# A two-block transformer kernel: squares of X moved behind the splits, tables loaded later

## Chip, core and metric

The kernel runs on one core of one Trainium2 chip. The metric is device time in microseconds (us) of one execution. The kernel before takes 1373.84 us, the median of 3 runs (1373.65 to 1375.49).

## What is computed

A 512 x 1024 activation `x` goes through two transformer blocks. The first is a mixer with a global and a windowed attention and a SiLU FFN, the second a pooling mixer, a stick-breaking attention, an FFN and a gated projection of a second input `p`. Only the opening matters here:

```
h = rms_norm(x, norm_mix_pre)        # x * rsqrt(mean(x*x) + EPS) * gain
proj = h @ w_in                      # 1024 -> 1536 columns
qa, ka, va, qb, kb, vb = split(proj)
qa, ka = rope(rms_norm(qa)), rope(rms_norm(ka));  qb, kb = rope(qb), rope(kb)
...                                  # attentions, FFN, the whole second block
x = x + sigmoid(rms_norm(x) @ w_ple_gate) * (p @ w_ple_proj)
```

## The kernel before

Everything is transposed: `X` holds 8 tiles of 128 features x 512 positions. Matrices are read in units of 16 blocks of 128x128 (`w_raw`, three slots in turn). For near-fp32 accuracy each operand is split into a high part of type fp32r (ScalarE, `w_hi`, `h_hi`) and the remainder (VectorE, `w_lo`, `h_lo`), and each product is three matmuls (`three`): hi x hi, lo x hi and hi x lo.

The order of work is written out by hand, one program for each engine, with semaphores between them. An engine executes its instructions strictly in that order, so an instruction that waits holds up all that stands behind it. The opening goes so:

- **SP** queues the loads: X in five parts (`X_PARTS`), between them the first weight unit in quarters, then units 1 and 2, all without a wait. Unit 3 waits until the matmuls of unit 0 are done.
- **ACT** (L906 to L934) loads gains, `ident` and `ones` on its own DMA queue. Then for each of 8 tiles it makes `h_hi[k] = X[k] * gain`, every second time the high part of a weight quarter, issues the load of `c1` after the first quarter (1.25 MiB: a matrix for head sums, one for rotation, attention masks, and cosines and sines), and squares the tile before. The squares go to the two buffers of `sq` in turn, so `square` waits at L866 until POOL has added the one two before. Behind the eighth come the load of `p` into `hf`, `split(1)` (the high part of unit 1), the high part of `p`, and rounded copies of `ident` and of the masks. Then the loop over the 12 output chunks evacuates (`evacuate`), splits later units and finishes heads.
- **POOL** adds squares 1 to 7 into `sqsum` (`sum_squares`, L418); the eighth is taken directly by TensorE.
- **DVE** makes `h_lo` and the low quarters, `split(1)`, the low part of `p`, `split(2)`, then the statistics (`variance`, `factors`), and from L1415 on the normed and rotated heads (`rope`), which share their cosine and sine tables in `c1`.
- **PE** runs `first_units` (chunks 0 and 1 together, feature tile by feature tile, as they arrive), then chunk 2 out of unit 1. After chunk 2 `beside(2)` calls `total`: with `ones` as right side it sums `sqsum` and the last square over partitions (16 matmuls of one column), and takes up `item(0)` and `item(1)` (a transpose, head sums, a rotation). Three feature tiles into chunk 3 `eps_row` makes the row that DVE waits for at L1415.

`F1`, which the change uses, is an 8-tile buffer that later holds the mixer's output. It lies where the query tiles `QA` lie, which are first written after the first rotated query.

Of the kernel before, what the change touches and what calls it, by code (L numbers as in the profile page):

```python
# [12 lines left out]
P = 128  # L13
KD = D // P
# [51 lines left out]
C1_AT = C_INVC + 4 * PADW  # L66
C_HONE, C_ROT, C_MASK = C1_AT, C1_AT + P, C1_AT + 2 * P
# [20 lines left out]
def build(nc, xT, pT, weights, gains, consts, outT):  # L88
# [5 lines left out]
    ACT = mybir.ActivationFunctionType  # L94
# [4 lines left out]
    with ctx:  # L99
# [258 lines left out]

        X_PARTS = [(0, 1), (1, 2), (2, 4), (4, 6), (6, 8)]

        def landed(u):
            return raw_landed[u % SLOTS], 16 * (u // SLOTS + (u % SLOTS > 0))

# [44 lines left out]
        @block.gpsimd  # L408
        def _(pool):
            def sum_squares(nm):  # L410

                if nm.before is not None:
                    pool.wait_ge(*nm.before.total(1))
                nc.gpsimd.memset(sqsum[:, :], 0.0).then_inc(nm.summed.sem, 1)
                for j in range(nm.sums - 1):
                    pool.wait_ge(*nm.squares(j + 1))
                    pool.wait_ge(*nm.summed(j + 1))
                    nc.gpsimd.tensor_tensor(sqsum[:, :], sqsum[:, :], sq[:, j % 2, :], ALU.add  # L418
                                            ).then_inc(nm.summed.sem, 1)

            def zero_masked(t):

                for at in (0, 512, 896, 1024):
                    v = t[:, at:at + P]
                    last = nc.gpsimd.affine_select(out=v, in_=v, compare_op=ALU.is_gt, fill=0.0, base=0,
                                                   pattern=[[1, P]], channel_multiplier=-1)
                return last

            n_self = [0]

            def link(ins):

                n_self[0] += 1
                ins.then_inc(pool_self, 1)
                pool.wait_ge(pool_self, n_self[0])

            def low_qk(j):

                c = ORDER1[j]
                last = None  # L440
                for i in range(2):
                    if last is not None:
                        link(last)
                    pool.wait_ge(roped_hi, 2 * ROPED.index(c) + i + 1)
                    rows, other = slice(HD * i, HD * i + HD), slice(HD * (1 - i), HD * (1 - i) + HD)
                    t = y_of(j)[rows, :]
                    if c in (4, 10):
                        k = KA if c == 4 else KB
                        hi = k[rows, 0, i, :]
                        link(nc.gpsimd.tensor_tensor(k[rows, 1, i, :], t, hi.bitcast(f32), ALU.subtract))  # L450
                        last = nc.gpsimd.tensor_tensor(k[other, 1, i, :], t, hi.bitcast(f32), ALU.subtract)
                    else:
                        q, h = (QA, 2 * c + i) if c in NORMED else (QB, 2 * (c - 6) + i)
                        last = nc.gpsimd.tensor_tensor(q[other, h, :], t, q[rows, h, :].bitcast(f32), ALU.subtract)
                last.then_inc(rope_done, 1)
                pool.wait_ge(rope_done, ROPED.index(c) + 1)

            sum_squares(n_mix_pre)
            for j in range(len(ORDER1)):
                if ORDER1[j] not in V1:  # L460
                    low_qk(j)
            for nm in norms[1:7]:
                sum_squares(nm)
            for h in range(NH):
                pool.wait_ge(sp_ready, h + 1)
                zero_masked(E2[:, h % 2, :]).then_inc(sp_masked, 1)
            for nm in norms[7:]:
                sum_squares(nm)
# [3 lines left out]
        def _(pe):  # L472
# [58 lines left out]
            def total(nm):  # L531

                if nm.before is None:
                    pe.wait_ge(c0_landed, 32)
                for src, ready, n in ((sqsum[:, :], nm.summed, nm.n), (sq[:, (nm.n - 1) % 2, :], nm.squares, nm.n)):
                    pe.wait_ge(*ready(n))
                    for b in range(NB):
                        last = mm(ps[:, nm.ss_bank, b:b + 1], src[:, b * P:(b + 1) * P], ones[:, 0:1],
                                  ready is nm.summed and b == 0, True, loose=True)
                last.then_inc(nm.total.sem, 1)  # L540
# [311 lines left out]
        def _(act):  # L852
# [8 lines left out]
            def af(out, in_, func, **kw):  # L861
                return nc.scalar.activation(out, in_, func, **kw)  # L862

            def split(u):

                slot, width = u % SLOTS, tiles_of(u)  # L866
                act.wait_ge(*landed(u))
                af(w_hi[slot][:, 0:width * P], w_raw[slot][:, 0:width * P], ACT.Copy).then_inc(hi_ready, 1)

            def square(nm, j, src):  # L870
                if j >= 2:
                    act.wait_ge(*nm.summed(j))
                af(sq[:, j % 2, :], src, ACT.Square).then_inc(nm.squares.sem, 1)

            def tables(name):

# [33 lines left out]
            for k in range(KD):  # L910
                if k < 2 or k % 2 == 0:
                    act.wait_ge(x_landed[k if k < 2 else k // 2 + 1], 16)
                af(h_hi[:, k, :], X[:, k, :], ACT.Copy, scale=gcol("norm_mix_pre", k)).then_inc(n_mix_pre.hi.sem, 1)
                if k % 2 == 0:
                    act.wait_ge(first_landed[k // 2], 16)
                    af(quarter(w_hi[0], k // 2), quarter(w_raw[0], k // 2), ACT.Copy).then_inc(first_hi, 1)
                if k == 0:
                    act.dma_start(c1[:, :], consts[:, C1_AT:]).then_inc(c1_landed, 16)
                else:
                    square(n_mix_pre, k - 1, X[:, k - 1, :])  # L920
            square(n_mix_pre, KD - 1, X[:, KD - 1, :])
            act.dma_start(hf[:, :, :], pT.rearrange("(k p) s -> p k s", p=P)).then_inc(p_landed, 16)
            split(1)
            act.wait_ge(p_landed, 16)
            af(p_hi[:, :, :], hf[:, :, :], ACT.Copy).then_inc(p_hi_ready, 1)


            def finish(j):
                c = ORDER1[j]
                if c in V1:  # L930
                    act.wait_ge(vtr_done, V1.index(c) + 1)
                    act.wait_ge(*n_mix_pre.diag(1))
                    for b in range(NB):
                        last = af((VA if c == 5 else VB)[:, b, :], ps[:, rot_bank(j), b * P:(b + 1) * P], ACT.Copy,  # L934
                                  scale=stat[:, 3, b:b + 1])
                    last.then_inc(v_ready, 1)
                elif c in NORMED:
                    act.wait_ge(hvar_ready, NORMED.index(c) + 1)
                    link(af(rt[:, 3, :], rt[:, 2, :], ACT.Ln))
                    af(rt[:, 3, :], rt[:, 3, :], ACT.Exp, scale=-0.5).then_inc(hguess_ready, 1)  # L940

            def high_qk(j):
# [13 lines left out]
                           ACT.Copy)  # L956
                    af(dst, y_of(j)[rows, :], ACT.Copy).then_inc(roped_hi, 1)

            act.wait_ge(c0_landed, 32)
            act.wait_ge(c1_landed, 16)  # L960
            af(ident_r[:, :], ident[:, :], ACT.Copy).then_inc(masks_ready, 1)
            af(mask_r[:, :, :], c1[:, C_MASK - C1_AT:C_MASK - C1_AT + 2 * P].rearrange("p (m c) -> p m c", m=2),
               ACT.Copy).then_inc(masks_ready, 1)

            def evacuate(j):

                c = ORDER1[j]
# [15 lines left out]
            for j in range(12):  # L983
                if j in (3, 5, 7, 9):
                    split(j // 2 + 2)
                evacuate(j)
                if j == 1:
                    split(2)
                if j == 2:
                    guess(n_mix_pre)  # L990
                    finish(0)
                    finish(1)
                if 3 <= j <= LATE1:
                    finish(j - 1)
                if 3 <= j < LATE1 + 2:
                    high_qk(j - 2)
# [247 lines left out]
        def _(dve):  # L1244
# [24 lines left out]
            def split(u):  # L1269

                slot, width = u % SLOTS, tiles_of(u)
                dve.wait_ge(hi_ready, u)
                low(w_lo[slot][:, 0:width * P], w_raw[slot][:, 0:width * P], w_hi[slot][:, 0:width * P]
                    ).then_inc(lo_ready, 1)
# [79 lines left out]
            for k in range(KD):  # L1354
                late_low(n_mix_pre, "norm_mix_pre", k)
                if k % 2 == 0:
                    dve.wait_ge(first_hi, k // 2 + 1)
                    low(quarter(w_lo[0], k // 2), quarter(w_raw[0], k // 2), quarter(w_hi[0], k // 2)
                        ).then_inc(first_lo, 1)
            split(1)  # L1360
            dve.wait_ge(p_hi_ready, 1)
            low(p_lo[:, :, :], hf[:, :, :], p_hi[:, :, :]).then_inc(p_lo_ready, 1)
            split(2)
            dve.wait_ge(c0_landed, 32)
            variance(n_mix_pre)
            dve.wait_ge(*n_mix_pre.var(1))
# [367 lines left out]
```

## Time and profile before

| | |
|---|---|
| median of 3 runs | 1373.84 us (1373.65 to 1375.49) |
| the profiled execution's own time | 1378.3 us |
| its span | 1376.5 us |
| mean granted TensorE clock | 0.988 |
| busy: PE, PEld, DVE, ACT, POOL | 97%, 78%, 50%, 40%, 11% of the span |

PE is the matmul pipe of TensorE, PEld its weight loads, DVE is VectorE, ACT ScalarE, POOL GpSimd, SP the engine that issues most DMAs; ACTq and SPq rows are their issues of DMAs. A name such as `ps<-h_hi,w_hi` is output and inputs; numbers of buffers are left out, and so `F1` is shown as `F`. The clock is a fraction of full speed. The two levels that occur are 0.50 (1.2 GHz) and 1.00 (2.4 GHz). In a bracket behind a row stands how long the engine was idle before it and what ended that.

### The profile page before, as it was taken

To read this page: it belongs to the slowest core of one execution; us is meant where nothing else is said; L and a number is where in the kernel's file an instruction comes from. 1 tells how busy PE (TensorE), PEld (TensorE's weight loads), DVE (VectorE), ACT (ScalarE), POOL (GpSimd) and SP (SyncE) were. 2 spreads that over 40 slices of the span, in tenths; PEclk is the share of its full clock that TensorE was granted. 3 is DMA by queue.
4 is the path that set the end of the run, shared out by engine and by line. 5 is a ranking of instruction groups with operands and counts; after the bars stand their busy time and mean duration, and the time that the engine had idled before them with its cause. 6 is when DMAs were issued, how large, how long until landed. Compare 5 with 4: busy or idle time off the path is not lost.

```text
span 1376.5 us, 14683 instructions
## 1 busy us (share of the span) xinstructions
PE 1329.5 (97%) x6056; PEld 1066.9 (78%) x6056; DVE 694.8 (50%) x907; ACT 546.1 (40%) x733; POOL 150.3 (11%) x136
## 2 busy tenths in 40 slices
PE   7987989999999999999999999999999999999995
PEld 5764657888888888887888777888888888888874
DVE  6998773665444442126534455563544354423254
ACT  6558864543233222225224555542423232222232
POOL 3351012510000000103000001012000000010021
PEclk9999989999999999999999999999999999999997
DMA  6110003122222222331321111233222223232311
GB/s 242 62 61 1 1 1 122 63 92 95 106 105 92 92 75 94 105 96 66 130 92 62 62 62 64 90 99 115 94 92 92 92 94 107 69 105 92 117 62 61
DMA packets 20594, 117.74 MB, mean 86 GB/s; under 512 B 2480, under 2 KB 2864, under 8 KB 9904
## 3 DMA queue, kind: packets, MB, share of 16 engines
q1 hardware_dynamic: 19680, 114.79, 23.8%
q10 hardware_dynamic: 848, 2.01, 0.4%
q8 instruction: 48, 0.79, 0.2%
q14 instruction: 18, 0.15, 0.0%
HBM read 114.70 MB, written 2.10 MB: 85 GB/s over the span
## 4 chain that ended last, share of the span: by engine, by line
PE 89%; DVE 7%; DMA 1%; ACT 1%; issue 1%; SPq 0%; POOLq 0%; POOL 0%; DVEq 0%
PE ps L474 87%; PE ps L675 2%; DVE rt L1264 1%; DVE w_lo L1257 1%; DMA w_raw<-weights 1%; DVE nmax L1430 1%; DVE F L1261 1%; DVE rt L1257 0%; DVE hf L1257 0%; DVE OUT L1264 0%; DVE h_lo L1264 0%; ACT w_hi L862 0%; DVE y L1257 0%; DVE y L1264 0%; DVE diag L1261 0%
## 5 line engine op out<-in xcount | busy, mean ns | idle before, releaser
L474 PE MATMUL ps<-h_hi,w_hi 128*128 128x512 f32 x1248 | 495.2, 397 | 13.2 <-DVE w_lo L1257 10.6
L474 PE MATMUL ps<-h_lo,w_hi 128*128 128x512 f32 x1248 | 487.4, 391 | 0.0
L474 PE MATMUL ps<-h_hi,w_lo 128*128 128x512 f32 x1248 | 487.2, 390 | 0.0
L1257 DVE TENSOR_TENSOR w_lo<-w_raw,w_hi 128x2048 fp32r<-128x2048 f32 (+2 forms) x117 | 246.4, 2109 | 266.8 <-ACT w_hi L862 266.8
L474 PEld LDWEIGHTS ps<-h_hi,w_hi 128*128 128x128 f32 x1248 | 235.2, 188 | 69.7 <-issue 13.8
L862 ACT ACTIVATE w_hi<-w_raw 128x2048 fp32r<-128x2048 f32 (+2 forms) x117 | 201.1, 1721 | 191.0 <-DMA w_raw<-weights 190.8
L474 PEld LDWEIGHTS ps<-h_lo,w_hi 128*128 128x128 f32 x1248 | 235.3, 189 | 51.0 <-issue 3.1
L474 PEld LDWEIGHTS ps<-h_hi,w_lo 128*128 128x128 f32 x1248 | 235.1, 188 | 49.7
L418 POOL TENSOR_TENSOR sqsum<-sqsum,sq 128x512 f32<-128x512 f32 x66 | 95.6, 1448 | 917.5 <-ACT sq L862 915.9
L474 PE MATMUL ps<-mid_hi,w_hi 128*128 128x512 f32 x352 | 136.9, 389 | 0.0
L474 PE MATMUL ps<-mid_lo,w_hi 128*128 128x512 f32 x352 | 136.9, 389 | 0.0
L474 PE MATMUL ps<-mid_hi,w_lo 128*128 128x512 f32 x352 | 136.9, 389 | 0.0
L1257 DVE TENSOR_TENSOR hf<-ps,factors_sb 128x512 f32<-128x512 f32 x56 | 38.6, 690 | 193.7 <-PE ps L474 193.6
L862 ACT ACTIVATE mid_hi<-hf 128x512 fp32r<-128x512 f32 x44 | 27.8, 633 | 209.8 <-DVE hf L1257 209.8
L474 PEld LDWEIGHTS ps<-mid_lo,w_hi 128*128 128x128 f32 x352 | 66.1, 188 | 13.8
L474 PEld LDWEIGHTS ps<-mid_hi,w_lo 128*128 128x128 f32 x352 | 66.1, 188 | 13.8
L474 PEld LDWEIGHTS ps<-mid_hi,w_hi 128*128 128x128 f32 x352 | 66.1, 188 | 13.5
L862 ACT ACTIVATE sq<-sq 128x512 f32<-128x512 f32 x44 | 27.7, 632 | 91.6 <-DVE sq L1257 91.6
L675 PEld LDWEIGHTS ps<-ident,F 128*128 128x128 f32 x208 | 23.9, 147 | 42.7 <-DVE F L1261 39.9
L862 ACT ACTIVATE h_hi<-X,gain 128x512 fp32r<-128x512 f32 x40 | 28.9, 722 | 61.1 <-DVE X L1257 58.4
L675 PE MATMUL ps<-ident,F 128*128 128x128 f32 x208 | 37.6, 297 | 15.2 <-DVE F L1261 15.0
L1430 DVE TENSOR_REDUCE nmax<-ps 128x1 f32<-128x512 f32 (+2 forms) x64 | 37.5, 587 | 17.9 <-PE ps L474 17.7
(187 smaller groups left out, 1188.0 us busy)
## 6 DMA issues: line engine op xcount, KB each, us to landing
w_raw<-weights SPq DMA_DIRECT2D x81, 1024.0 KB, 4.8
w_raw<-weights SPq DMA_DIRECT2D x32, 704.0 KB, 3.9
out_t<-OUT SPq DMA_DIRECT2D x8, 256.0 KB, 2.0
X<-x_t SPq DMA_DIRECT2D x3, 512.0 KB, 7.4
c<-constants ACTq DMA_DIRECT2D x1, 1280.0 KB, 8.8
w_raw<-weights SPq DMA_DIRECT2D x4, 256.0 KB, 8.4
wp_raw<-weights SPq DMA_DIRECT2D x1, 1024.0 KB, 7.0
X<-x_t SPq DMA_DIRECT2D x2, 256.0 KB, 4.1
```

Of the source, the lines that this page charges most:

```text
L418: nc.gpsimd.tensor_tensor(sqsum[:, :], sqsum[:, :], sq[:, j % 2, :], ALU.add).then_inc(nm.summed.sem, 1)
L474: return nc.tensor.matmul(out, lhsT, rhs, start=start, stop=stop, skip_group_check=loose)
L675: last = nc.tensor.transpose(ps[:, 3 + s % 2, (kb - k0) * P:(kb - k0 + 1) * P], prob[:, s % 3, (kb - k0) * P:(kb - k0 + 1) * P], ident[:, :])
L862: return nc.scalar.activation(out, in_, func, **kw)
L1257: return nc.vector.tensor_tensor(out, a, b, op)
L1261: else nc.vector.tensor_scalar(out, a, s1, None, op0))
L1264: return nc.vector.scalar_tensor_tensor(out=out, in0=a, scalar=s, in1=b, op0=op0, op1=op1)
L1430: nc.vector.tensor_reduce(nmax[:, s:s + 1], ps[:, s % 3, at:end], AX.X, ALU.max, negate=True).then_inc(nmax_ready, 1)
```

## The change

- The squares of X's eight tiles are made after all parts `h_hi` and the quarters, and after `split(1)`. They go to eight tiles of `F1` and so wait for nothing.
- The load of `c1` is issued behind the last `h_hi`, not after the first weight quarter.
- The high part of `p` is made after `split(2)`, and the low part after DVE's `split(2)`.
- The rounded copies of `ident` and the masks are made after chunk 3 is evacuated.

```diff
+        def square_of(nm, j):
+            return F1[:, j, :] if nm is n_mix_pre else sq[:, j % 2, :]
...
-                    nc.gpsimd.tensor_tensor(sqsum[:, :], sqsum[:, :], sq[:, j % 2, :], ALU.add
+                    nc.gpsimd.tensor_tensor(sqsum[:, :], sqsum[:, :], square_of(nm, j), ALU.add
...
-                for src, ready, n in ((sqsum[:, :], nm.summed, nm.n), (sq[:, (nm.n - 1) % 2, :], nm.squares, nm.n)):
+                for src, ready, n in ((sqsum[:, :], nm.summed, nm.n), (square_of(nm, nm.n - 1), nm.squares, nm.n)):
...
             def square(nm, j, src):
-                if j >= 2:
+                if j >= 2 and nm is not n_mix_pre:
                     act.wait_ge(*nm.summed(j))
-                af(sq[:, j % 2, :], src, ACT.Square).then_inc(nm.squares.sem, 1)
+                af(square_of(nm, j), src, ACT.Square).then_inc(nm.squares.sem, 1)
...
-                if k == 0:
-                    act.dma_start(c1[:, :], consts[:, C1_AT:]).then_inc(c1_landed, 16)
-                else:
-                    square(n_mix_pre, k - 1, X[:, k - 1, :])
-            square(n_mix_pre, KD - 1, X[:, KD - 1, :])
+            act.dma_start(c1[:, :], consts[:, C1_AT:]).then_inc(c1_landed, 16)
+            split(1)
+            for k in range(KD):
+                square(n_mix_pre, k, X[:, k, :])
             act.dma_start(hf[:, :, :], pT.rearrange("(k p) s -> p k s", p=P)).then_inc(p_landed, 16)
-            split(1)
-            act.wait_ge(p_landed, 16)
-            af(p_hi[:, :, :], hf[:, :, :], ACT.Copy).then_inc(p_hi_ready, 1)
...
                 if j == 1:
                     split(2)
+                    act.wait_ge(p_landed, 16)
+                    af(p_hi[:, :, :], hf[:, :, :], ACT.Copy).then_inc(p_hi_ready, 1)
...
             split(1)
+            split(2)
             dve.wait_ge(p_hi_ready, 1)
             low(p_lo[:, :, :], hf[:, :, :], p_hi[:, :, :]).then_inc(p_lo_ready, 1)
-            split(2)
```

How the instructions stand: ScalarE, from the sixth tile on, before.

```order
L862 ACTIVATE h_hi<-X,gain 128x512
L862 ACTIVATE sq<-X 128x512 [waits norm_summed]
L862 ACTIVATE h_hi<-X,gain 128x512 [waits x_landed4]
L862 ACTIVATE w_hi<-w_raw 128x512 [waits first_landed3]
L862 ACTIVATE sq<-X 128x512 [waits norm_summed]
L862 ACTIVATE h_hi<-X,gain 128x512
L862 ACTIVATE sq<-X 128x512 [waits norm_summed] x2
L922 DMA hf<-p_t 128x2x512
L862 ACTIVATE w_hi<-w_raw 128x2048 [waits raw_landed1]
L862 ACTIVATE p_hi<-hf 128x1024 [waits p_landed]
L862 ACTIVATE ident_r<-ident 128x128 [waits c1_landed,c0_landed]
L862 ACTIVATE mask_r<-c 128x256
```

The same stretch of ScalarE with the change (`F` is `F1`).

```order
L865 ACTIVATE h_hi<-X,gain 128x512 [waits x_landed4]
L865 ACTIVATE w_hi<-w_raw 128x512 [waits first_landed3]
L865 ACTIVATE h_hi<-X,gain 128x512
L920 DMA c<-constants 128x2560
L865 ACTIVATE w_hi<-w_raw 128x2048 [waits raw_landed1]
L865 ACTIVATE F<-X 128x512 x8
L924 DMA hf<-p_t 128x2x512
L865 ACTIVATE y<-ps 128x512 [waits group_done]
L865 ACTIVATE ysq<-ps 128x512 [waits group_done]
L865 ACTIVATE y<-ps 128x512
L865 ACTIVATE w_hi<-w_raw 128x2048 [waits raw_landed2]
L865 ACTIVATE p_hi<-hf 128x1024 [waits p_landed]
```

The squares have lost their waits and stand in one block behind the high part of unit 1; `p_hi` stands behind unit 2.

VectorE around the split of unit 1, before and with the change.

```order
L1264 SCALAR_TENSOR_TENSOR h_lo<-X,gain,h_hi 128x512 [waits norm_hi]
L1257 TENSOR_TENSOR w_lo<-w_raw,w_hi 128x2048 [waits hi_ready]
L1257 TENSOR_TENSOR p_lo<-hf,p_hi 128x1024 [waits p_hi_ready]
L1257 TENSOR_TENSOR w_lo<-w_raw,w_hi 128x2048 [waits hi_ready]
L1260 TENSOR_SCALAR stat<-ps 128x4 [waits norm_total,c0_landed]
```

```order
L1265 SCALAR_TENSOR_TENSOR h_lo<-X,gain,h_hi 128x512 [waits norm_hi]
L1258 TENSOR_TENSOR w_lo<-w_raw,w_hi 128x2048 [waits hi_ready] x2
L1258 TENSOR_TENSOR p_lo<-hf,p_hi 128x1024 [waits p_hi_ready]
L1261 TENSOR_SCALAR stat<-ps 128x4 [waits norm_total,c0_landed]
L1261 TENSOR_SCALAR rt<-ident,stat 128x128 [waits norm_var]
```

The low part of `p` now stands between unit 2's and the variance.

## Rows read from the trace of the kernel before

**Rows 1.** The page: its span, and the engines' shares of the chain that ended last.

```profile
span 1376.5 us, 14683 instructions
...
PE 89%; DVE 7%; DMA 1%; ACT 1%; issue 1%; SPq 0%; POOLq 0%; POOL 0%; DVEq 0%
```

**Rows 2.** Busy time by stretch: PE, PEld, DVE, ACT, POOL, clock, DMA share, GB/s.

```profile
37.60:80.00 42.40, 39.05 (x153) 28.17 (x151) 41.48 (x40) 22.50 (x31) 17.81 (x12) 1.00 0.22 75
...
215.00:620.00 405.00, 404.65 (x1788) 333.90 (x1788) 172.67 (x183) 133.01 (x149) 35.50 (x25) 1.00 0.27 94
```

**Rows 3.** The chain that ended last, 0 to 60 us: start us, us, what.

```profile
20.48 11.92 PE ps L474 x52
...
32.90 4.66 PE ps L474 x15
...
37.65 0.70 DVE sqsum L1415
```

**Rows 4.** Timeline of PE: start us, us, instruction, count, idle before.

```profile
12.07 0.39 PE L474 MATMUL ps<-h_hi,w_hi 128*128 128x512 f32 x1
...
14.59 0.39 PE L474 MATMUL ps<-h_hi,w_lo 128*128 128x512 f32 x1
...
20.48 0.47 PE L474 MATMUL ps<-h_hi,w_hi 128*128 128x512 f32 x1 [1.80 <-DVE w_lo L1257]
...
24.81 0.63 PE L474 MATMUL ps<-h_hi,w_hi 128*128 128x512 f32 x1
...
30.56 0.95 PE L474 MATMUL ps<-ones,sqsum 128*128 128x1 f32 x8
```

**Rows 5.** Timeline of ACT, 5 to 22 us.

```profile
5.64 0.34 ACTq L918 DMA_DIRECT2D c<-constants  x1
...
19.82 0.63 ACT L862 ACTIVATE sq<-X 128x512 f32<-128x512 f32 x1 [0.84 <-POOL sqsum L418]
...
20.35 1.90 ACT L862 ACTIVATE w_hi<-w_raw 128x2048 fp32r<-128x2048 f32 x1
```

**Rows 6.** Timeline of POOL: the last four adds, and an operation beside a short DVE one.

```profile
15.13 6.35 POOL L418 TENSOR_TENSOR sqsum<-sqsum,sq 128x512 f32<-128x512 f32 x4 [1.48 <-ACT sq L862]
...
47.45 1.28 POOL L450 TENSOR_TENSOR KA<-y,KA 64x512 fp32r<-64x512 f32 x1 [25.97 <-ACT KA L862]
```

**Rows 7.** Timeline of DVE.

```profile
4.83 0.75 DVE L1264 SCALAR_TENSOR_TENSOR h_lo<-X,gain,h_hi 128x512 fp32r<-128x512 f32 x1 [4.83 <-ACT h_hi L862]
...
22.29 2.29 DVE L1257 TENSOR_TENSOR w_lo<-w_raw,w_hi 128x2048 fp32r<-128x2048 f32 x1 [0.26 <-ACT w_hi L862]
...
52.61 3.38 DVE L1257 TENSOR_TENSOR w_lo<-w_raw,w_hi 128x2048 fp32r<-128x2048 f32 x1
```

**Rows 8.** DMA: X issued at 3.17, a quarter 3.64, c 5.64, unit 1 6.02.

```profile
X<-x_t SPq DMA_DIRECT2D x1, 512.0 KB, 7.4
...
w_raw<-weights SPq DMA_DIRECT2D x1, 256.0 KB, 10.2
...
c<-constants ACTq DMA_DIRECT2D x1, 1280.0 KB, 8.8
...
w_raw<-weights SPq DMA_DIRECT2D x1, 1024.0 KB, 12.6
```

**Rows 9.** DMA throughput, 0 to 30 us in 40 slices of 0.75 us.

```profile
GB/s 0 0 55 296 280 234 254 328 388 358 352 382 456 445 448 393 448 355 396 470 404 461 415 437 426 382 98 25 30 385 270 0 0 0 87 109 426 393 382 0
```

**Rows 10.** Stretches around two idle times of PE, columns as in rows 2.

```profile
18.50:22.00 3.50, 1.70 (x7) 1.05 (x6) 3.50 (x3) 2.66 (x3) 2.84 (x2) 0.99 0.44 175
22.00:25.20 3.20, 3.20 (x8) 2.34 (x8) 2.94 (x3) 1.97 (x5) 0.00 (x0) 0.50 0.33 126
...
78.00:80.00 2.00, 0.22 (x1) 0.00 (x0) 1.92 (x3) 1.09 (x2) 0.00 (x0) 1.00 0.00 0
80.00:82.00 2.00, 1.96 (x5) 1.01 (x6) 1.95 (x3) 1.26 (x2) 1.21 (x1) 1.00 0.00 0
```

**Rows 11.** Timeline of PE at the end: half of the last total, at clock 0.50.

```profile
1360.78 1.86 PE L474 MATMUL ps<-ones,sqsum 128*128 128x1 f32 x8 [4.56 <-POOL sqsum L418]
```

More of the change, by code:

```diff
@@ L957, in high_qk @@
                     af(dst, y_of(j)[rows, :], ACT.Copy).then_inc(roped_hi, 1)
[L959 to L963, printed above, removed]
             def evacuate(j):
@@ L992, in _ @@
                     finish(1)
+                if j == 3:
+                    act.wait_ge(c0_landed, 32)
+                    act.wait_ge(c1_landed, 16)
+                    af(ident_r[:, :], ident[:, :], ACT.Copy).then_inc(masks_ready, 1)
+                    af(mask_r[:, :, :], c1[:, C_MASK - C1_AT:C_MASK - C1_AT + 2 * P].rearrange("p (m c) -> p m c", m=2),
+                       ACT.Copy).then_inc(masks_ready, 1)
                 if 3 <= j <= LATE1:
```

## The prediction, made before the changed kernel ran

> **What bounds the kernel now.** I began with the chain of waits. TensorE carries 89% of it, VectorE 7% [rows 1]; what a change at the start is worth depends on which engine the chain is on there. The busy times by stretch say it: from 37.6 to 80 us VectorE works 41.48 of 42.4 us, and later, from 215 to 620 us, TensorE 404.65 of 405 [rows 2]. So the head work is a VectorE queue that starts at 37.65 with the copy of the eps row, and all behind it moves by as much as that start does. The chain into it [rows 3] runs over TensorE alone from 20.48: unit 0's last matmuls, chunk 2, the total at 30.56 [rows 4], items 0 and 1, a third of chunk 3, the eps row. The question is thus when TensorE begins `total`, and at what clock it then runs. A difference of 0.2% (2.7 us) is about what a measurement of this kernel can tell from none.
>
> TensorE starves before that point. It stands 1.80 us idle before 20.48 for `w_lo` [rows 4], since VectorE gets its high parts late and runs slowly; and chunk 2 begins at 24.81 only, since ScalarE turns to unit 1 at 20.35, behind the squares, the last of which even waited 0.84 us for POOL [rows 5].
>
> **The tables.** The part of X issued at 3.17 lands 7.4 us later, at 10.57; the quarter issued right behind it lands only at 3.64 + 10.2 = 13.84 [rows 8]. In between 1.25 MiB of tables pass (landing 5.64 + 8.8 = 14.44). At some 420 GB/s [rows 9] they cost 3.1 us. Moved back, the third quarter lands near 10.9, and unit 1, which landed at 6.02 + 12.6 = 18.6, at 15.5. The tables are issued near 13.5. The load of `p`, with nothing in its way, was issued beside the square at 19.82 [rows 5] and its bytes begin at 21.75 [rows 9]; so the tables' begin after 15.4, when unit 1's bytes are through, and land by 21 with unit 2. `item(0)` and VectorE need them near 30: no cost.
>
> **Split and squares.** Without squares between them ScalarE has the eighth `h_hi` at about 14.2 (seven more parts and three quarters of 0.5 to 0.7 us, held by the landings). It splits unit 1 from 15.5 to 17.4 (1.90, [rows 5]). The squares take 0.53 us each (19.82 to 20.35, [rows 5]), from 17.4 to 21.6, the first done at 18.0. Nothing waits for a slot of `sq` any more. The four moved conversions (`p_hi`, two roundings, and VectorE's `p_lo`) are worth nothing on the path: `p_lo` ends near 29.5, before the total is ready, and the roundings (0.6 us) fit into ScalarE's idle time beside the first ropes. If that cover were gone, they would cost their own length.
>
> **TensorE up to chunk 2.** Eleven steps from 12.07 to 14.59 give 0.229 us a matmul [rows 4]. `h_lo` takes 0.75 with POOL idle [rows 7], so VectorE is ahead from here on, and the 36 matmuls of tiles 2 to 7 run through: 12.07 + 8.2 = 20.3. VectorE has the low part of unit 1 at 17.4 + 2.29 to 3.38 [rows 7], so 19.7 to 20.8, and chunk 2 (24 matmuls, 5.5 us) ends near 26.2. TensorE thus reaches `total` 4.4 us earlier than before.
>
> **The adds.** POOL cannot follow. It now starts at 18.1 and has seven adds: beside a busy VectorE four took 6.35 us, 1.6 each; with VectorE hardly in the way the nearest row is 1.28, with a gap 1.36 [rows 6]. Both ends: 27.6 (all 1.36) and 29.3 (all 1.6). I take four slow ones, beside the splits of units 1 and 2, and three fast ones in the gap between: 18.1 + 6.4 + 4.1 = 28.6. The total then starts at 28.6 in place of 30.56: **2.0 us earlier**, bounds 1.3 and 3.0. The adds have become the wait.
>
> The Trainium skill has a rule against this step: GPSIMD Engine Reference, Specifications, says that GpSimd shares its SBUF interfaces with VectorE and that VectorE instructions with two SBUF inputs contend. By it the change puts all its adds beside splits, which have two SBUF inputs, and the sum would be the end at 29.3 where they lie beside one all the time. The trace agrees on VectorE's side (`w_lo` 2.29 against 3.38).
>
> **The clock.** TensorE now stands idle from 26.2 to 28.6, then issues 16 one-column matmuls. In the trace 1.80 us idle, with TensorE busy 1.70 of 3.5 us, were followed by a stretch of 3.2 us at 0.50, that is 1.2 GHz; yet 1.8 us idle up to 80.04 were followed by 1.00 [rows 10]. So 2.4 us idle plus 1.7 us of little work probably, not surely, bring a stretch at 0.50. Its price: half a total took 0.95 us at 1.00 and 1.86 at 0.50 [rows 4, 11], and dense work in a stretch of 3.2 us loses 1.6. Both ways about 1.7 us for one stretch; 0 if it falls into the idle time alone, 3.4 if a second follows. I take one: 1.7.
>
> **Sum:** -2.0 + 1.7 = -0.3 us at the eps copy, carried to the end unchanged. The profiled execution took 1378.3 us, 4.5 more than the median of the runs, and I apply the difference to the median: 1373.84 - 0.3 = 1373.5 us.
>
> **The rivals.**
> 1. *The clock stays at 1.00.* For it: the idle time before 80.04. Then the whole 2.0 us stay, with quick adds 3.0: 1370.8 to 1371.8. Chance 0.21.
> 2. *Two low stretches.* For it: the total at 0.50 takes 3.5 us and is itself little work. -2.0 + 3.4 gives 1375.2; with the adds at 29.3, 1375.9. Chance 0.16.
> 3. *The tables go in front of unit 1* and not behind it (the other side). The quarter that landed at 13.84 shows that they can take nearly all of the DMA engines' time. If their bytes start before unit 1's are through, near 14.2, unit 1 lands up to 3.1 us later than I say, at 18.6, squares and adds move by as much, the total starts at 31.7, 1.1 later than before, and with one low stretch it is +2.8, 1376.6; with two +4.5. The point from which it decides: a start of the tables' bytes within 0.7 us of their issue. Against it: the 1.9 us of `p`. Chance 0.12. The Trainium skill (DMA: Bandwidth & Descriptors, Queues, rings and completion order) says that an engine goes round robin between queues by packets. By that rule only half of the rate would go to the tables; unit 1 would land some 1.5 us late, and the time would be 1375. Of the 0.12 a third is this.
> 4. *The change does nothing at all*, since the start of the head work is made up for later, or something in the 60 us behind eats it: 1373.8. VectorE's 41.48 of 42.4 us speak against it. Chance 0.06.
>
> **Numbers.** Forecast 0.45. Rivals 0.21, 0.16, 0.12, 0.06. Faster by over 0.2% needs -2.75 us: half of rival 1, 0.11. Slower by over 0.2%: most of rival 3 and a tail of rival 2, 0.11. The rest, 0.78, lies within. The range takes the forecast with its bounds and the bulk of rivals 1 to 3: 1371.2 to 1376.4.
>
> **What would show it.** Unit 1's split on ScalarE at 15.5 us and squares until 21.6; no idle time of TensorE from 12 to 26; an idle time of about 2.4 us before `ones,sqsum`, ended by POOL, at 28.6; a clock of 0.50 in some 3 us after it; the eps copy near 37.3; VectorE as full as before up to about 80. I am wrong if unit 1 is split later than 17, if the adds end before TensorE arrives, or if the eps copy's shift is not found again at the end.

## The result, and the profile after

The change is slower: 1381.9 us, the median of 20 runs (1377.33 to 1384.78), against 1376.66 us in 20 runs of the kernel before (1373.65 to 1378.9). The ratio is 1.0036, with a 95% interval of 1.0029 to 1.0043, so some 5 us were lost, where I had forecast 0.3 us of gain and drawn the range to 1376.4. (The three runs shown before the prediction lay low, at 1373.84; more runs put that kernel at 1376.7, which already lies above my range. So 2.8 us of the distance between 1381.9 and my 1373.5 are the base and not the change; the change's own part is +5.2 us against the -0.3 forecast.)

The page of the changed kernel: its span and the engines' shares of the chain. POOL has come into it; before it had 0% [rows 1].

```profile
span 1380.3 us, 14683 instructions
...
PE 88%; DVE 7%; POOL 1%; DMA 1%; issue 1%; ACT 1%; SPq 0%; POOLq 0%; DVEq 0%
```

The chain that ended last, 0 to 60 us, which answers to [rows 3] (start us, us, what).

```profile
15.59 0.42 ACT w_hi L865
...
18.10 2.89 POOL sqsum L421
21.03 0.09 issue
21.13 1.30 POOL sqsum L421
...
25.43 3.14 POOL sqsum L421
...
28.70 2.07 POOL sqsum L421
...
30.90 1.27 POOL sqsum L421
...
32.30 3.55 PE ps L477 x16
...
43.82 0.70 DVE sqsum L1416
```

From 18.1 to 32.2 the chain lies on POOL's adds. What bounded the kernel before there, TensorE, is on it only from the total on. The eps copy, which I had called the point that sets the rest, comes at 43.82 and not at 37.65: 6.17 us late. TensorE's timeline splits this in two.

```profile
32.30 1.84 PE L477 MATMUL ps<-ones,sqsum 128*128 128x1 f32 x8 [6.68 <-POOL sqsum L421]
34.00 1.84 PE L477 MATMUL ps<-ones,F 128*128 128x1 f32 x8
...
36.60 1.92 PE L477 MATMUL ps<-ysq,c 128*128 128x512 f32 x2
...
42.70 1.02 PE L477 MATMUL ps<-rt,ones 128*128 128x512 f32 x2
```

The total starts 1.74 us late (32.30 against 30.56, [rows 4]), behind 6.68 us of idle time. And from its start to the copy it is 11.52 us instead of 7.09: 4.43 us more for the same instructions. That is the clock. Busy time and granted clock by stretch, with the columns of rows 2:

```profile
22.00:25.20 3.20, 3.20 (x15) 2.65 (x15) 0.25 (x1) 3.20 (x5) 2.91 (x3) 1.00 0.67 282
25.20:28.60 3.40, 0.42 (x2) 0.00 (x1) 3.40 (x2) 1.63 (x3) 3.21 (x2) 0.86 0.00 0
28.60:32.00 3.40, 0.00 (x0) 0.00 (x0) 1.03 (x1) 0.00 (x0) 3.16 (x2) 0.50 0.00 0
32.00:35.40 3.40, 3.10 (x15) 3.13 (x15) 0.00 (x0) 0.00 (x0) 0.16 (x1) 0.50 0.02 5
35.40:38.80 3.40, 3.40 (x10) 2.21 (x10) 2.31 (x12) 0.71 (x4) 0.00 (x0) 0.50 0.00 0
38.80:42.00 3.20, 3.20 (x8) 1.91 (x7) 0.00 (x0) 0.84 (x4) 0.00 (x0) 0.61 0.00 0
```

The clock is at 0.50 (1.2 GHz) from about 28 to 41 us. In [rows 10] it was so for one stretch only, from 22 to 25.2.

Then the timelines of POOL and VectorE, side by side, say why the adds were late.

```profile
18.10 2.88 POOL L421 TENSOR_TENSOR sqsum<-sqsum,F 128x512 f32<-128x512 f32 x1 [16.78 <-ACT F L865]
...
21.13 1.29 POOL L421 TENSOR_TENSOR sqsum<-sqsum,F 128x512 f32<-128x512 f32 x1
...
25.43 3.13 POOL L421 TENSOR_TENSOR sqsum<-sqsum,F 128x512 f32<-128x512 f32 x1
...
28.70 2.06 POOL L421 TENSOR_TENSOR sqsum<-sqsum,F 128x512 f32<-128x512 f32 x1
```

```profile
17.54 2.29 DVE L1258 TENSOR_TENSOR w_lo<-w_raw,w_hi 128x2048 fp32r<-128x2048 f32 x1 [2.29 <-ACT w_hi L865]
24.95 2.48 DVE L1258 TENSOR_TENSOR w_lo<-w_raw,w_hi 128x2048 fp32r<-128x2048 f32 x1 [5.12 <-ACT w_hi L865]
27.36 2.28 DVE L1258 TENSOR_TENSOR p_lo<-hf,p_hi 128x1024 fp32r<-128x1024 f32 x1
```

The first add starts at 18.10, while the split of unit 1 runs until 19.83, and ends 1.15 us after that, at 20.98. The add of 25.43 ends 1.1 us behind the split of unit 2 (27.43 and 28.56). Then `p_lo`, begun at 27.36, waits for that add: 2.28 us instead of the 1.23 of the kernel before. The add of 28.70 waits for `p_lo` in turn. Read so, no operation is slow here: one of the two stands still until the other has finished its whole instruction. The kernel before has the same on VectorE's side: a 128x512 operation beside POOL's adds took 1.75 us, where 0.69 is its time alone. Its rows for that, and for `p_lo` with POOL idle:

```profile
18.59 1.75 DVE L1257 TENSOR_TENSOR w_lo<-w_raw,w_hi 128x512 fp32r<-128x512 f32 x1
...
24.58 1.23 DVE L1257 TENSOR_TENSOR p_lo<-hf,p_hi 128x1024 fp32r<-128x1024 f32 x1
```

Behind the copy the loss stays. To the first `nmax` of the attention it is 62.12 us before and 62.11 after. The attention itself took 110.66 and 108.94 us in these two executions, at a mean clock of 0.94 and 0.95; everything behind it 1166.07 and 1165.43. So 6.17 - 0.01 - 1.72 - 0.64 = 3.80 us, the difference of the spans (1380.3 and 1376.5).

### The profile page after: what moved, and what is told of

Read it like the earlier page. It is cut to its first block, busy times and chain, and to the rows that moved or that the text cites. A ratio compares the mean times of both kernels' runs of the same rounds, so it can differ in the third digit from the quotient of the medians.

```text
span 1380.3 us, 14683 instructions
## 1 busy us (share of the span) xinstructions
PE 1328.6 (96%) x6056; PEld 1067.4 (77%) x6056; DVE 690.0 (50%) x907; ACT 545.9 (40%) x733; POOL 153.3 (11%) x136
## 4 chain that ended last, share of the span: by engine, by line
PE 88%; DVE 7%; POOL 1%; DMA 1%; issue 1%; ACT 1%; SPq 0%; POOLq 0%; DVEq 0%
PE ps L477 87%; PE ps L678 2%; DVE rt L1265 1%; POOL sqsum L421 1%; DMA w_raw<-weights 1%; DVE w_lo L1258 1%; DVE F L1262 1%; DVE nmax L1431 1%; DVE rt L1258 0%; DVE hf L1258 0%; DVE OUT L1265 0%; ACT w_hi L865 0%; DVE y L1258 0%; DVE y L1265 0%; DVE diag L1262 0%
## 5 line engine op out<-in xcount | busy, mean ns | idle before, releaser
L421 POOL TENSOR_TENSOR sqsum<-sqsum,sq 128x512 f32<-128x512 f32 x59 | 85.3, 1446 | 907.0 <-ACT sq L865 906.0
```

The source lines that it names most:

```text
L421: nc.gpsimd.tensor_tensor(sqsum[:, :], sqsum[:, :], square_of(nm, j), ALU.add).then_inc(nm.summed.sem, 1)
```

## The experiments

In each group of experiments the kernel before ran again, with medians of 1376.34 to 1376.96 us, and the ratios are to those runs. Where a time is set against the change, it is against the change's 20 runs above. "The copy" is the copy of the eps row in the profiled execution.

Theories at this point: **L** (A in the expectations written first), that POOL's adds and VectorE's splits exclude each other and the adds thereby became the wait; **C**, that the clock's fall is a price of its own, larger than the wait; against them rival **B**, that adds out of `F1` are slow by themselves, rival **D**, that the clock costs nothing (in total_later: that it falls whatever stands there), and rival **F**, that the late tables are to blame.

### splits_away: no splits beside the adds

```diff
             split(1)
-            split(2)
-            dve.wait_ge(p_hi_ready, 1)
-            low(p_lo[:, :, :], hf[:, :, :], p_hi[:, :, :]).then_inc(p_lo_ready, 1)
...
             factors(n_mix_pre)
+            split(2)
+            dve.wait_ge(p_hi_ready, 1)
+            low(p_lo[:, :, :], hf[:, :, :], p_hi[:, :, :]).then_inc(p_lo_ready, 1)
```

> The change, but VectorE splits unit 2 and p behind the factors of the first norm, so that only unit 1's split runs beside POOL's adds. Theory A (adds and VectorE's splits hold each other up, and the late adds are the wait): the six adds behind the first take 1.3 to 1.4 us each, the last ends near 29.3 instead of 32.2, the eps copy comes 2.5 to 3.5 us earlier than in the change (40.5 to 41.5), the time is 1.5 to 3.5 us under the change's. Rival B (adds out of F1 are slow by themselves, because of where F1 lies or of eight tiles in a row): the adds still end near 32 and nothing is gained.

Measured: 1379.29 us (12 runs), ratio to the kernel before 1.0013 (1.0003 to 1.0024), 2.6 us under the change. POOL's seven adds and the total in the timelines:

```profile
17.85 11.43 POOL L421 TENSOR_TENSOR sqsum<-sqsum,F 128x512 f32<-128x512 f32 x7 [16.52 <-ACT F L865]
```

```profile
29.43 1.84 PE L477 MATMUL ps<-ones,sqsum 128*128 128x1 f32 x8 [3.47 <-POOL sqsum L421]
```

The adds end at 29.28, as theory A had it, with the operands where they were: rival B falls. The copy comes at 39.70, 4.1 us earlier than in the change and 0.8 us earlier than I had expected at best.

### quarters: is it the whole instruction?

```diff
                 dve.wait_ge(hi_ready, u)
+                if u in (1, 2):
+                    for q in range(4):
+                        last = low(quarter(w_lo[slot], q), quarter(w_raw[slot], q), quarter(w_hi[slot], q))
+                    last.then_inc(lo_ready, 1)
+                    return
```

> The change, with VectorE's splits of units 1 and 2 each as four instructions of 128x512 instead of one of 128x2048. Theory L (an add on POOL and a VectorE instruction with two SBUF inputs exclude each other for the length of the whole instruction; who comes second waits): the first add, which took 2.89 us beside the long split, takes at most 1.3 + 0.6 = 1.9 us, and the quarters take up to 0.6 + 1.2 us beside adds; the split of unit 1 ends up to 2 us later, the last add 1 to 2 us earlier than 32.2. Rival G (both share the rate, as I had taken it): each add takes 1.6 and the quarters 0.85 us, without any of 1.9.

Measured: 1377.36 us (10 runs), ratio 1.0007 (0.9998 to 1.0017). POOL's adds and VectorE's quarters in the timelines:

```profile
17.90 1.30 POOL L421 TENSOR_TENSOR sqsum<-sqsum,F 128x512 f32<-128x512 f32 x1 [16.58 <-ACT F L865]
...
19.35 1.54 POOL L421 TENSOR_TENSOR sqsum<-sqsum,F 128x512 f32<-128x512 f32 x1
...
21.03 1.53 POOL L421 TENSOR_TENSOR sqsum<-sqsum,F 128x512 f32<-128x512 f32 x1
```

```profile
17.95 1.80 DVE L1258 TENSOR_TENSOR w_lo<-w_raw,w_hi 128x512 fp32r<-128x512 f32 x1
...
19.67 1.77 DVE L1258 TENSOR_TENSOR w_lo<-w_raw,w_hi 128x512 fp32r<-128x512 f32 x1
...
21.36 1.75 DVE L1258 TENSOR_TENSOR w_lo<-w_raw,w_hi 128x512 fp32r<-128x512 f32 x1
```

A quarter alone takes 0.69; beside adds 1.75 to 1.80, its own time and what was left of an add. The first add has gone from 2.88 to 1.30. Rival G's 0.85 is nowhere: it is exclusion by instruction, and the length of VectorE's instruction decides who pays. Here the last add ends at 29.1 and the total starts at 29.25; the four quarters took 5.78 us in place of 2.29, so TensorE stood 2.78 us idle ahead of chunk 2 instead. Both moved further than I had expected, the last add by 3.1 us and the end of unit 1's split by 3.3. That the edit took 4.5 us off the change, with no work taken away, is the strongest evidence for L.

The copy comes at 38.06 only, since here too the clock fell, though not behind the 2.78 us of idle time (which ended at 23.17) but behind the total:

```profile
22.00:25.00 3.00, 1.83 (x8) 1.51 (x9) 1.37 (x2) 3.00 (x4) 2.71 (x3) 1.00 0.75 306
...
31.00:34.00 3.00, 3.00 (x11) 1.56 (x10) 2.61 (x13) 0.56 (x3) 0.00 (x0) 0.72 0.00 0
```

### warm: the clock by itself

```diff
                 if nm.before is None:
                     pe.wait_ge(c0_landed, 32)
+                    for i in range(28):
+                        mm(ps[:, EPS_BANK, :], w_hi[1][:, i % 8 * P:(i % 8 + 1) * P], h_hi[:, i % 8, :], i == 0, i == 27)
```

> The change, with 28 matmuls into a free bank ahead of the total, whose result nobody reads: TensorE stands idle no more while the adds go on (28 x 0.229 = 6.4 us, until about 32), and the total starts where it did, at 32.3. Theory C (the clock at 0.50 after the idle time costs the larger part): clock 1.00 from 28 to 42, total 1.7 and not 3.4 us, eps copy at 32.3 + 7.1 = 39.4 instead of 43.8, the time 4.4 us under the change's, within 2 us of before. Rival D (the late start costs it all and the clock nothing): the time of the change stays.

Measured: 1379.56 us (12 runs), ratio 1.0019 (1.0009 to 1.0029), an interval that just touches the change's: 2.3 us under the change. Timeline of the total, then the stretches behind it:

```profile
32.74 1.05 PE L477 MATMUL ps<-ones,sqsum 128*128 128x1 f32 x8 [0.35 <-POOL sqsum L421]
```

```profile
31.00:34.00 3.00, 2.65 (x19) 2.07 (x17) 0.00 (x0) 0.00 (x0) 1.55 (x2) 1.00 0.00 0
34.00:37.00 3.00, 3.00 (x13) 2.20 (x13) 1.97 (x11) 0.41 (x2) 0.00 (x0) 0.58 0.00 0
37.00:40.00 3.00, 3.00 (x10) 1.84 (x9) 0.33 (x2) 1.14 (x4) 0.00 (x0) 0.85 0.00 0
```

The instructions added are pure waste, the total starts no earlier, and the copy still comes 2.2 us earlier: rival D falls. But half of my number was missing. Half the total now runs at full speed (1.05 against 1.84), yet from about 34 to 37 the clock is at 0.50 all the same, and the copy comes at 41.64 and not 39.4. TensorE had hardly idled; what it had done just before the fall were the 16 one-column matmuls.

### total_later: useful work in the gap

```diff
-                if j == 2:
-                    total(n_mix_pre)
-                if j == 3:
-                    factor(n_mix_pre)
-                for i in (0, 1) if j == 2 else (j - 1,) if j <= LATE1 else ():
+                if j == 3:
+                    total(n_mix_pre)
+                if j == 4:
+                    factor(n_mix_pre)
+                for i in (0, 1) if j == 2 else () if j == 3 else (2, 3) if j == 4 else (j - 1,) if j <= LATE1 else ():
...
-                unit("in1", u, 2 * u, 2, KS, h_hi, h_lo, after=beside, hooks={3: {3: eps_row}})
+                unit("in1", u, 2 * u, 2, KS, h_hi, h_lo, after=beside, hooks={4: {2: eps_row}})
```

> The change, with items 0 and 1 and chunk 3's matmuls ahead of the total, and the eps row in chunk 4: useful dense work stands where TensorE waited for POOL. Theory C (the idle time brought the clock down): TensorE idle under 1 us before the total, which starts at 32.3 at 1.00; eps copy near 36.5, 7 us before the change's and 1 us before that of the kernel before; ratio to the kernel before 0.998 to 1.001. Rival D (the clock falls by itself there): a copy near 40.

Measured: 1376.93 us (12 runs), ratio 1.0003 (0.9994 to 1.0011). The adds end as late as in the change, the total starts at 33.42 with no idle time ahead of it, the clock stays at 1.00 through the next stretches, and the copy is at 37.73 (1.2 us later than I had said, since chunk 3's matmuls ended 1.1 us after 32.3). The same late adds cost next to nothing once dense matmuls stand before and behind the total. Filling the gap ahead of it alone, as in warm, gave back only half.

### tables_only and tables_back: the load of the tables

tables_only is the kernel before with the late load alone, the edit shown; tables_back is the change with the early load.

```diff
-                if k == 0:
-                    act.dma_start(c1[:, :], consts[:, C1_AT:]).then_inc(c1_landed, 16)
-                else:
+                if k:
                     square(n_mix_pre, k - 1, X[:, k - 1, :])
+            act.dma_start(c1[:, :], consts[:, C1_AT:]).then_inc(c1_landed, 16)
             square(n_mix_pre, KD - 1, X[:, KD - 1, :])
```

> The kernel before with one part of the change: the load of the tables moved behind the last high part of X; squares stay between the parts. Theory A: the third weight quarter lands near 11, no idle time of TensorE of 1.8 us before 20; squares and POOL's adds, one by one beside VectorE, end near 19.5, unit 1 is split 2 us earlier, the total starts at about 28.5 without a wait, and the eps copy 2 us earlier than before: 1.5 to 2.5 us under the kernel before. Rival F (moving the tables costs something): at or above the kernel before.

Measured: 1376.36 us (12 runs), ratio 0.9996 (0.9986 to 1.0005), with the copy at 36.13, 1.5 us earlier. The gain I expected in the time is within the interval only at its edge; the runs do not show it.

> The change with its tables' load put back behind the first weight quarter. Theory: the tables' 3.1 us of transfers come before the third quarter again, unit 1 lands at 18.6, its split, the squares and all adds start 3 us later, the total at 35.3 and the eps copy near 45 to 47; 1 to 3 us slower than the change. Rival F (the late tables are what makes the change slow): the eps copy comes earlier than in the change.

Measured: 1384.81 us (4 runs), ratio 1.0055 (1.0038 to 1.0073). Unit 1 is split at 18.58, the total starts at 35.31 behind 6.66 us of idle time, the copy comes at 45.46. All of it as expected, and rival F falls: the late tables bring the copy 1.6 us forward within this change, and 2.9 us in the medians, where the two intervals just overlap. In the change the third quarter, issued at 3.64, landed 7.5 us later and unit 1 9.7 us later:

```profile
w_raw<-weights SPq DMA_DIRECT2D x1, 256.0 KB, 7.5
...
w_raw<-weights SPq DMA_DIRECT2D x1, 1024.0 KB, 9.7
```

### interleaved: the squares' place

```diff
                 if k % 2 == 0:
                     act.wait_ge(first_landed[k // 2], 16)
                     af(quarter(w_hi[0], k // 2), quarter(w_raw[0], k // 2), ACT.Copy).then_inc(first_hi, 1)
+                if k:
+                    square(n_mix_pre, k - 1, X[:, k - 1, :])
             act.dma_start(c1[:, :], consts[:, C1_AT:]).then_inc(c1_landed, 16)
+            square(n_mix_pre, KD - 1, X[:, KD - 1, :])
             split(1)
-            for k in range(KD):
-                square(n_mix_pre, k, X[:, k, :])
```

> The change, with the squares between the high parts as in the kernel before, but in the eight tiles of F1, and the last ahead of unit 1's split. Theory A (it is the squares' place behind the split of unit 1 that makes the adds late): adds from 8 to about 20, next to VectorE's short operations; unit 1 split from 18; total at 28 to 29 without a wait at 1.00; eps copy at 35.5 to 36.5, 7 to 8 us before the change's. Rival B (adds out of F1 are slow): copy above 38.

Measured: 1376.95 us (10 runs), ratio 1.0004 (0.9995 to 1.0013): with the squares back between the high parts the loss is gone, though they still go to `F1`. The copy came at 38.10 in the profiled execution, just where I had put rival B, but not for B's reason. The adds ended at 20.42, six of them in 9.77 us, 1.63 each, as out of `sq` (1.59, [rows 6]). TensorE idled 1.81 us before 21.12 for VectorE, as before, and the clock fell behind it:

```profile
22.00:25.00 3.00, 3.00 (x10) 2.33 (x9) 1.84 (x1) 0.60 (x1) 0.00 (x0) 0.56 0.01 3
```

tables_only idled 1.79 us at the same place (before 20.68) and kept 1.00 in that stretch:

```profile
22.00:25.00 3.00, 3.00 (x15) 2.32 (x14) 1.56 (x2) 1.26 (x3) 0.00 (x0) 1.00 0.41 153
```

From the end of the gap to the total it is 9.89 us here and 8.36 there. So the same kind of gap costs now 1.5 us, now nothing.

### p_back: the split of p

```diff
             act.dma_start(hf[:, :, :], pT.rearrange("(k p) s -> p k s", p=P)).then_inc(p_landed, 16)
+            act.wait_ge(p_landed, 16)
+            af(p_hi[:, :, :], hf[:, :, :], ACT.Copy).then_inc(p_hi_ready, 1)
...
             split(1)
-            split(2)
             dve.wait_ge(p_hi_ready, 1)
             low(p_lo[:, :, :], hf[:, :, :], p_hi[:, :, :]).then_inc(p_lo_ready, 1)
+            split(2)
```

> The change with the splits of p put back (the high part on ScalarE ahead of chunk 0's evacuation, the low part on VectorE ahead of unit 2's). Theory L (adds and VectorE's splits exclude each other for whole instructions, and the sum of both is what counts): the same instructions lie beside the adds in another order, the last add ends within 1 us of 32.2, the time within 1.5 us of the change's. Rival I (splitting p later is what collides with the adds): the last add ends 2 us earlier and the time falls by 2 us or more.

Measured: 1382.43 us (4 runs), ratio 1.0050 (1.0035 to 1.0066), which overlaps the change's interval. The last add ends at 31.39 and the copy comes at 42.64; the seven adds take 14.10 us from first to last, against 14.06 in the change. Moving the split of `p` is no part of the loss that can be measured.

### shared_adds, two_halves, two_halves_eps: the way out

If POOL's adds are the wait, VectorE, idle from 19.83 to 24.95 in the change, can take some. In shared_adds it adds squares 4, 5 and 6 and the total takes three sums; in two_halves it adds 4 to 7 and the total takes two. The edit of two_halves:

```diff
-                self.sums = n + (kind == "wide")
+                self.sums = 5 if before is None else n + (kind == "wide")
...
-                for src, ready, n in ((sqsum[:, :], nm.summed, nm.n), (square_of(nm, nm.n - 1), nm.squares, nm.n)):
+                second = ((F1[:, 4, :], Count(half_summed), 3) if nm.before is None else
+                          (square_of(nm, nm.n - 1), nm.squares, nm.n))
+                for src, ready, n in ((sqsum[:, :], nm.summed, nm.sums), second):
...
             split(1)
+            for i in (5, 6, 7):
+                dve.wait_ge(*n_mix_pre.squares(i + 1))
+                if i > 5:
+                    dve.wait_ge(half_summed, i - 5)
+                tt(F1[:, 4, :], F1[:, 4, :], F1[:, i, :], ALU.add).then_inc(half_summed, 1)
             split(2)
```

> The change, with POOL adding squares 0 to 3 only, VectorE adding 4, 5 and 6 in its idle time between the splits of units 1 and 2, and the total taking three sums (8 more one-column matmuls, 0.9 us). Theory A: POOL is done near 25.2, VectorE near 22.5, TensorE reaches the total at 25.5 without a wait and at clock 1.00; the eps copy comes at 25.5 + 7.1 + 0.9 = 33.5, 4.1 us before that of the kernel before, and the time is 3 to 5 us under the kernel before (ratio 0.9965 to 0.998). Rival E (a shift of the eps copy does not reach the end, since something in between gives it back): the eps copy comes at 33.5, but the time is within 1 us of the kernel before.

Measured: 1375.51 us (11 runs), ratio 0.9988 (0.9978 to 0.9998), 1.5 us under the kernel before and not 3 to 5. TensorE reached the total at 26.04 without idling, but behind its 24 small matmuls the clock fell (0.77 and 0.66 in the stretches 28 to 31 and 31 to 34), and the copy came at 35.69, 2.2 us later than expected.

> As shared_adds, but VectorE adds squares 4 to 7 (three adds), so that the total takes two sums of 16 one-column matmuls as before, and not 24. Theory C with small matmuls counting as little work: in shared_adds the clock fell to 0.50 from 29 to 33 behind the 24 of them without any idle time; with 16, as in the kernel before, it stays at 1.00: total at 26.0, eps copy at 33.1 and not 35.7; ratio to the kernel before 0.9965 to 0.9975. Rival H (the fall depends on when the small matmuls lie and not on their number): it falls here in some runs too, eps copy near 35, ratio 0.9985.

Measured: 1373.04 us (12 runs), ratio 0.9974 (0.9965 to 0.9982). The profiled execution had the fall all the same (0.71 and 0.72), copy at 35.18: rival H has a share. 16 small matmuls are not safe either. It was, at 1375.11, nearly the longest of the 12 runs, so in others the fall may not have come, or something behind the start went faster; no profile shows it.

two_halves_eps is two_halves with `hooks={3: {1: eps_row}}`.

> two_halves, and the eps row after one feature tile of chunk 3 and not after three. Theory A (what counts is when the eps copy comes): 6 matmuls less stand before it, 1.4 us at 1.00 or 2.6 at 0.50, and what it needs from VectorE was ready at 31.3; copy near 33.0 to 33.8, 1.4 to 2.2 us before two_halves', ratio to the kernel before 0.996 to 0.997. Rival E (VectorE's queue is not the bound so early): the ratio of two_halves, 0.9974, stays.

Measured: 1371.71 us (5 runs, 1371.32 to 1372.69), ratio 0.9968 (0.9955 to 0.9980): faster than both kernels. Timelines of PE and of VectorE:

```profile
26.01 0.95 PE L477 MATMUL ps<-ones,sqsum 128*128 128x1 f32 x8
26.82 1.03 PE L477 MATMUL ps<-ones,F 128*128 128x1 f32 x8
30.59 1.02 PE L477 MATMUL ps<-rt,ones 128*128 128x512 f32 x2
```

```profile
31.72 0.69 DVE L1423 COPY sqsum<-ps 128x512 f32<-128x512 f32 x1 [0.73 <-PE ps L477]
```

The clock stayed at 1.00 from 16 to 46 us in this execution, and the copy came at 31.72, 5.9 us before the kernel before; the median is 4.6 us under it. I had expected 33.0 at best, since I had started from a copy that the clock had delayed. The intervals of this run and of two_halves overlap, so the times alone do not show that the earlier eps row gained anything, and rival E is not excluded. From copy to first `nmax` it is 63.11 us here and 62.0 to 62.1 in all other runs: an earlier eps row begins to leave a little behind.

## Why the prediction was wrong

- **What bounds the start: right.** The copy of the eps row sets the rest. In 13 executions with copies from 31.72 to 45.46 us, the first `nmax` followed after 62.01 to 62.14 us, but for the one of 63.11. The medians follow too: from the kernel with the earliest copy to the one with the latest the copy moves by 13.7 us and the median by 13.1 (1371.71 to 1384.81).
- **Tables and unit 1: right.** 15.5 forecast for unit 1's split, 15.59 measured; third quarter 10.9 and 11.14; rival 3 did not occur, since the tables, issued at 13.15, let unit 1 pass: their queue moved nothing from there until 16 us, when unit 1 had landed (15.6). The half rate that I gave them in that rival, if the queues take turns by packets, was too low: in the kernel before, from 10 to 13 us, the tables' queue moved 0.35 MB in each us and SP's 0.07 to 0.08, in 34 to 36 packets against 37 to 42. The turns were nearly alike in number and not in bytes.
- **TensorE up to chunk 2: right.** It would have begun the total at 26.2; it was free at about 25.6. There was no idle time of note from 12 us on.
- **The adds: this step failed.** I had put the last at 28.6, with bounds of 27.6 and 29.3, and it ended at 32.17. I had read the four adds of [rows 6] as "1.6 us each beside a busy VectorE", a rate. They lay beside 128x512 operations, and what made the rate was an exclusion: beside a whole split an add took 1.6 to 1.8 us more than its 1.29 (2.88 and 3.13). I even had the other half of it in hand: `w_lo` took 3.38 us beside POOL [rows 7], which is 2.29 and the rest of an add. Nor did I see that `p_lo`, which I had costed at nothing, would lie beside the adds too, though moving it back gained nothing (p_back). The Trainium skill has the rule in full: SBUF — State Buffer, SBUF: two separate sides, calls the shared port pair an exclusive lock that whichever starts first holds for the whole instruction. The traces agree: 2.88 us for a 1.29 us add, 1.80 for a 0.69 us quarter. The row of the Trainium skill's GPSIMD Engine Reference, Specifications, that I had weighed only says that there is contention, and I turned it into a mean price.
- **The clock: the mechanism right, the size wrong.** I had charged one stretch of 3.2 us, 1.7 us in all. It was 0.50 for some 13 us, 4.43 us. The idle time was 6.7 us and not 2.4, and a total at 0.50 prolongs itself. My rival of two low stretches would have given 3.4. What the profiled executions do not settle is when it falls at all: not behind 2.78 us of idle time in quarters, but behind 1.81 us in interleaved.
- **The sum.** -2.0 + 1.7 was in truth +1.74 + 4.43 = +6.17 at the copy. The slower side had only a second low stretch and the tables as its mechanisms; that the adds themselves go past 30.56 I had excluded by bounds taken from one kind of neighbour.

How the loss divides is shown by single edits: without the squares' move it is gone (interleaved, 1.0004); without the long instructions beside the adds most of it is (quarters, 1.0007), and without the gap on TensorE too (total_later, 1.0003). The parts overlap and do not add up.

## What to carry to other kernels

When adds on GpSimd are moved, look at which VectorE instructions they come to lie beside and how long each of them is: a mean taken beside short ones says nothing beside long ones. Where a wait on TensorE can't be avoided, put dense matmuls that are due anyway in front of it and behind it: here the late start cost 1.7 us and the clock 4.4. And a sum that is the last thing before a wait is worth sharing between two engines.

## What the runs showed of the hardware

- The clock fell without idle time of note. In warm, quarters and two_halves it went to 0.50 behind 16 matmuls of one column, in shared_adds behind 24, with at most 0.35 us of idle time directly ahead of them. That it does not always do so is seen in the kernel before, in total_later and in two_halves_eps. What settles it in one execution was not tried.
- The attention took 105.0 us in one execution at a mean clock of 1.00 (tables_back), and 106.2 to 110.7 us at 0.98 to 0.94 in the others, with hardly a difference in VectorE's busy time (85.80 us against 85.86). This can account for up to 5.7 of the 5 to 7 us by which runs of one kernel differ. The two profiled executions with the shortest attention, tables_back and splits_away, were also the shortest of their kernels' runs. So it is why the spans of two profiled executions are a poor measure of a change at the start:

```profile
107.60:212.60 105.00, 89.32 (x537) 56.20 (x535) 85.80 (x247) 84.35 (x222) 14.04 (x13) 1.00 0.00 1
```

```profile
99.80:210.40 110.60, 95.27 (x536) 60.19 (x534) 85.86 (x247) 84.68 (x222) 13.98 (x13) 0.94 0.00 1
```

The first is the attention of tables_back, the second that of the kernel before.
